# Eight more tokens gathered row by row, waits reordered, and half of a query projection made for both token groups at once

## The chip, the cores and the metric

One core of a Trainium2 chip runs the whole kernel. The time is device microseconds of one execution. All data are fp32; a matrix multiplication of 128x128 weights shows as two LDWEIGHTS and two MATMUL records in the trace.

## What is computed

One layer of a decoder for 320 tokens: 256 of a prompt and 64 of eight requests (eight each). Cut to what matters here:

```python
def one_block(xb):                                    # PEER: product-key experts
    q = (xb @ w_pq).reshape(TOKEN_BLOCK, PEER_HEADS, PEER_DKEY)     # 8 heads x 256
    s1 = jnp.einsum('thd,kd->thk', q[..., :half], sub_k1)
    s2 = jnp.einsum('thd,kd->thk', q[..., half:], sub_k2)
    v1, i1 = lax.top_k(s1, PEER_TOPK)
    v2, i2 = lax.top_k(s2, PEER_TOPK)
    ...
    eidx = jnp.take_along_axis(cidx, pos, axis=-1)     # 16 of 16384 experts a head
    gate = jax.nn.softmax(best.astype(jnp.float32), axis=-1)
    u = expert_u[eidx]
    act = jax.nn.gelu(jnp.einsum('td,thkd->thk', xb, u).astype(jnp.float32), approximate=False)
    vv = expert_v[eidx]
    return jnp.einsum('thk,thkd->td', (gate * act).astype(xb.dtype), vv)
```

Before it come two attention mixers with an output projection (`w_out`), and cross-attention of four heads to 256 memory tokens (`w_cq`, `w_co`), each behind an RMSNorm; a final RMSNorm follows.

## The kernel before

Tokens are columns, 16 blocks of 128 features (`KT`). Group 0 (`FIRST_TILE`) is the first 128 tokens, group 1 (`THE_REST`) the other 192. Weights stream in chunks of 1 MB (128 x 2048) through a ring `WR` of four slots, loaded by SP in the order of `STREAM`; SP loads a slot again when PE has used it (`s_used`).

The stages, in PE's order:

- Projections and prompt attention, then request attention, eight iterations `n` (keys and values of a request are loaded by POOL into single buffers). Among the parts of an iteration PE makes the output tiles, cross queries and cross outputs of group 0 (`out_tile`, `cq_tile`, `co_tile` with group 0), into banks 5 and 6 by turns. DVE adds each to the residual stream in `XT` (`add_to_stream`, L891), behind `softmax_s(n + 1)`. `turn_s(n)` is the transposition of an iteration.
- Group 1: 16 `out` tiles, 4 `cq`, a loop over cross-attention (`scores_c`, `turn_c`, `values_c`, ten steps), 16 `co`. The query tiles of the experts for group 0 (`pq_tile(0, f)`, 16 of 128 columns) are set among them; those of group 1 (`pq_tile(1, f)`, 192 columns) follow. So each chunk of `w_pq` is loaded twice. The memory keys `km` and values `vm` of the requests come in two halves of four requests.
- Experts. For group 0 (128 tokens) every chosen expert row is fetched by an indirect DMA: row n of the list holds one expert for each of 128 partitions, 1 MB. POOL issues them (L539 for `expert_u`, L545 for `expert_v`), three or four in flight; DVE makes a dot product from each `u` row (`u_dot`, L1240) and adds each `v` row with its weight (`v_row`, L1253). There are 128 such rows for group 0. 16 more (`FEW`) hold the first 16 tokens of group 1, as 16 tokens x 8 heads on the partitions, with `h_few` as their input.
- The other 176 tokens (`DENSE`) go through all experts: 128 chunks of `uT` (`dense_u`, into four banks, gelu by ScalarE), then 128 chunks of `expert_v` (`dense_v`), 16 multiplications of 176 columns each. The gates are applied by maps: for chunks 100 to 123 (`MAP_LO` to `MAP_HI`) DVE makes one-hots (`one_hots`), PE multiplies them (`gate_maps`), DVE and ScalarE apply them, four tokens to a group. The choices of those tokens are transposed on PE at chunk 92 (`TURN`, `s_turn`); DVE copies them (`turned`, `s_turnev`) when it has done 141 row dots (`ROWS_BEFORE`), and the first map waits for this.
- In the maps DVE does one row dot or row sum a chunk, two at each third.
- The sum of the 16 tokens' rows is put into PSUM by 16 small multiplications with `pick` at `expert_v` chunk 96 (`FEW_OUT`).

Choosing the experts is DVE's work, in parts (`choose_part`: sub-keys, sums, experts) for one or two heads, set by hand between row dots (`next_row`). POOL can't issue a row before the experts of its heads are chosen (`s_idx`), nor rows 128 on before the choices of the 16 tokens were spread by ScalarE's DMAs (`s_few`), behind chunk 80.

Of the kernel before, what the change touches and what calls it, by code (L numbers as in the profile page):

```python
# [26 lines left out]
P = 128  # L27
D = 2048
# [28 lines left out]
FEW = 16  # L57
REST = NT - P
DENSE = REST - FEW
# [6 lines left out]
ROWS = SLOTS + FEW  # L66
# [10 lines left out]
FEW_OUT = 96  # L77
# [7 lines left out]
def tiles_of(stage, g, lo, hi):  # L85
# [69 lines left out]
def build(nc, d):  # L155
    with ExitStack() as ctx:
# [11 lines left out]
        BIG = region("BIG", NCH * DENSE + (URING + 2) * D)  # L168
# [84 lines left out]
        vm = [BIG[:, at:at + 1024] for at in (4096, 13440, 22528, 23552)]  # L253
# [4 lines left out]
        h_few = BIG[:, NCH * DENSE:NCH * DENSE + D]  # L258
        u_ring = [BIG[:, NCH * DENSE + (1 + r) * D:NCH * DENSE + (2 + r) * D] for r in range(URING)]
        h_tok = BIG[:, NCH * DENSE + (URING + 1) * D:NCH * DENSE + (URING + 2) * D]  # L260
# [43 lines left out]
        def tile_out(stage, g, f):  # L304
            if g == FIRST_TILE:
                at = f % 2 if stage == "pq" else 5 + f % 2
            else:
                at = (2, 3, 7)[f % 3] if stage in ("out", "co") else 2 + f % 2
            return bank[at][:, 0:WIDTH[g]]
# [58 lines left out]
        s_dev = sem("dense_gelu")  # L368
        s_vlast = sem("v_finished")
# [47 lines left out]
        def _(sp):  # L417
# [44 lines left out]
            def mem_values(g):  # L462
                for n in range(4):
                    sp.dma_start(vm[n], d["vm"][4 * g + n]).then_inc(s_vm[g], 16)

            for chunk in STREAM:
                pos, (stage, g, f) = POS[chunk], chunk
                before = pos - WR_N
                if before == POS["out", 1, 15]:
                    sp.wait_ge(s_used, FREED["out", 1, 15])  # L470
                    mem_keys(0)
                    mem_values(0)
                if before == POS["pq", 0, 10]:
                    sp.wait_ge(s_cS, V_REQ[0] + 1)
                    mem_keys(1)
                if before == POS["pq", 0, 12]:
                    sp.wait_ge(s_cV, 1)
                    mem_values(1)
# [23 lines left out]
        def _(pool):  # L502
# [28 lines left out]
            for n in range(ROWS):  # L531
# [3 lines left out]
                else:  # L535
                    pool.wait_ge(s_few, 16 * PH)
# [11 lines left out]
        def _(act):  # L548
# [160 lines left out]
            def keep_query(g, f):  # L709
# [27 lines left out]
            for k in range(2, 9):  # L737
                square(THE_REST, CROSS, k)
            for f in range(4, 8):
                keep_query(FIRST_TILE, f)  # L740
            for k in range(9, KT):
                square(THE_REST, CROSS, k)
                if k == 9:
                    keep_scores(2)
            keep_query(FIRST_TILE, 8)
            root(THE_REST, CROSS)
            keep_query(FIRST_TILE, 9)
            for it in range(7):
# [8 lines left out]
                if it < 4:  # L757
                    keep_query(FIRST_TILE, 10 + it)
            keep_scores(3)
            for k in range(KT):  # L760
                square(THE_REST, FFN, k)
            keep_query(FIRST_TILE, 14)
            root(THE_REST, FFN)
            keep_query(FIRST_TILE, 15)
            keep_scores(4)
            for f in range(KT):
                keep_query(THE_REST, f)
                if f == 1:
                    keep_rows(3, h_few, big)
            for c in range(OF_FIRST, len(GROUPS)):  # L770
# [1318 lines left out]
```

## Time and profile before

| | |
|---|---|
| median of 3 runs | 2308.41 us (2307.99 to 2311.57) |
| profiled execution, its own time | 2311.11 us |
| its span | 2309.2 us |
| TensorE busy | 2207.9 us, 96% |
| VectorE busy | 1179.1 us, 51% |
| ScalarE busy, GpSimd busy | 301.2 us, 386.3 us |
| moved by DMA | 843.21 MB, mean 365 GB/s |
| mean granted TensorE clock | 0.984 |

Busy time of PE counts each matmul to its modelled end, so PE looks busy also where it goes on slowly. A stretch is read from its DMA share, the number of PE records in it and who waits for whom.

### The profile page before, as it was taken

Reading aid. Unit: us, or ns where it says so; the run is one execution under the profiler, and the core shown is the slowest. Engines: PE = TensorE matmul, PEld = TensorE weight load, DVE = VectorE, ACT = ScalarE, POOL = GpSimd, SP = SyncE. Lnnn points to the kernel's source line nnn. Section 1 sums busy time; section 2 is a strip of 40 time slices with the busy share of each in tenths; the row PEclk is TensorE's granted clock in tenths of the full one; section 3 lists DMA queues with packets and bytes.
Section 4 is the critical chain, followed back from the end, with each engine's and each line's share of the span. In section 5 each row is a group of like instructions: output and inputs, shape, how many; then the busy total and the mean of one; then the engine's idle time right before and its main releaser. Section 6 shows DMA issues by size and latency. Waiting matters only on the chain.

```text
span 2309.2 us, 35404 instructions
## 1 busy us (share of the span) xinstructions
PE 2207.9 (96%) x14282; PEld 2015.7 (87%) x14282; DVE 1179.1 (51%) x2095; ACT 301.2 (13%) x926; POOL 386.3 (17%) x414
## 2 busy tenths in 40 slices
PE   7999998789889879999999999999999999999998
PEld 5677776577589868999999999899999999999998
DVE  3200003833566647767777544599744444444422
ACT  2000001722221012011111110144200000000000
POOL 0100000022302011232212221133311111111100
PEclk9999999999999989999999999999999999999999
DMA  7999982289959898999999999999999999999974
GB/s 280 405 413 381 385 316 81 80 333 357 398 201 396 345 383 315 407 398 422 422 421 420 420 420 420 372 372 376 402 422 421 422 422 421 422 422 422 421 315 155
DMA packets 117787, 843.21 MB, mean 365 GB/s; under 512 B 14432, under 2 KB 16608, under 8 KB 30656
## 3 DMA queue, kind: packets, MB, share of 16 engines
q1 hardware_dynamic: 62752, 485.30, 52.4%
q0 software_dynamic: 54128, 354.58, 37.7%
q10 hardware_dynamic: 816, 2.11, 0.2%
q8 instruction: 58, 0.95, 0.2%
q14 instruction: 33, 0.27, 0.0%
HBM read 834.25 MB, written 74.78 MB: 394 GB/s over the span
## 4 chain that ended last, share of the span: by engine, by line
PE 64%; DMA 23%; DVE 8%; issue 2%; ACT 1%; POOL 1%; SPq 0%; DVEq 0%; POOLq 0%; ACTq 0%
PE low L1414 39%; PE big L1414 24%; DMA BIG<-expert_u,VB 20%; DVE BIG L1240 4%; DMA WR<-wall 1%; DMA BIG<-kaT 1%; ACT BIG L630 1%; DMA BIG<-expert_v,VB 1%; DMA BIG<-memT 0%; DMA BIG<-va 0%; DVE CST L968 0%; POOL BIG L525 0%; DVE BIG L846 0%; PE low L1538 0%; DVE HT L883 0%
## 5 line engine op out<-in xcount | busy, mean ns | idle before, releaser
L1414 PE MATMUL low<-HT,WR 128*128 128x176 f32 (+3 forms) x6336 | 1081.9, 333 | 8.4 <-DMA WR<-wall 7.0
L1414 PEld LDWEIGHTS low<-HT,WR 128*128 128x128 f32 x6336 | 984.2, 191 | 98.2 <-issue 9.7
L1414 PE MATMUL big<-BIG,WR 128*128 (+3 forms) x2888 | 450.7, 312 | 11.3 <-DVE XT L891 7.1
L1253 DVE SCALAR_TENSOR_TENSOR XT<-BIG,VB,XT 128x2048 f32<-128x2048 f32 x128 | 300.9, 2351 | 302.7 <-DMA BIG<-expert_v,VB 302.4
L1414 PE MATMUL low<-BIG,WR 128*128 (+3 forms) x2616 | 434.8, 321 | 12.6 <-DMA WR<-wall 10.3
L1414 PEld LDWEIGHTS big<-BIG,WR 128*128 128x128 f32 x2888 | 419.3, 193 | 30.1 <-issue 18.5
L1240 DVE SCALAR_TENSOR_TENSOR BIG<-BIG 128x2048 f32<-128x2048 f32 x144 | 329.5, 2291 | 210.8 <-DMA BIG<-expert_u,VB 209.7
L1414 PEld LDWEIGHTS low<-BIG,WR 128*128 128x128 f32 x2616 | 411.0, 192 | 17.8 <-issue 10.5
L539 POOL DMA_INDIRECT BIG<-expert_u,VB x144 | 161.5, 1122 | 683.8 <-DVE BIG L1240 609.5
L545 POOL DMA_INDIRECT BIG<-expert_v,VB x144 | 161.5, 1122 | 558.2 <-DVE XT L1253 477.3
L914 DVE TENSOR_SCALAR BIG<-low 128x320 f32 x32 | 15.7, 492 | 264.0 <-PE low L1414 264.0
L1414 PE MATMUL big<-BIG 128*32 128x256 f32 (+4 forms) x868 | 80.5, 376 | 16.1 <-issue 8.9
L1414 PEld LDWEIGHTS big<-BIG 128*32 128x32 f32 (+2 forms) x868 | 52.7, 141 | 36.5 <-issue 14.6
L777 ACT ACTIVATE BIG<-low 128x176 f32 x100 | 31.8, 318 | 334.3 <-PE low L1414 324.2
L819 ACT ACTIVATE HT<-XT 128x2048 f32<-128x2048 f32 x1 | 1.9, 1910 | 557.1 <-DVE XT L1253 557.1
L793 ACT ACTIVATE HT<-HT,VB 128x128 f32<-128x128 f32 x176 | 56.2, 390 | 89.9 <-DVE HT L1354 89.9
L1354 DVE TENSOR_TENSOR HT<-CST,VB 128x512 f32<-128x512 f32 x88 | 56.6, 684 | 7.7 <-PE big L1414 7.7
L1414 PE MATMUL big<-HT 128*128 128x128 f32 x352 | 47.9, 280 | 5.0 <-ACT HT L793 5.0
L1414 PEld LDWEIGHTS big<-HT 128*128 128x128 f32 x352 | 45.5, 194 | 5.6 <-issue 5.5
L511 POOL DMA_DIRECT2D HT<-kbT x1 | 0.5, 536 | 266.8 <-PE low L1414 266.8
L525 POOL DMA_DIRECT2D BIG<-kaT x56 | 29.8, 539 | 81.2 <-PE low L1414 81.2
L622 ACT ACTIVATE BIG<-low 128x512 f32<-128x512 f32 (+3 forms) x5 | 2.3, 466 | 293.3 <-PE low L1500 293.3
(230 smaller groups left out, 1124.0 us busy)
## 6 DMA issues: line engine op xcount, KB each, us to landing
WR<-uT SPq DMA_DIRECT2D x128, 1024.0 KB
WR<-expert_v SPq DMA_DIRECT2D x128, 1024.0 KB
WR<-wall SPq DMA_DIRECT2D x122, 1024.0 KB
BIG<-va POOLq DMA_DIRECT2D x48, 512.0 KB, 11.0
BIG<-kaT POOLq DMA_DIRECT2D x64, 384.0 KB, 11.0
BIG<-kmT SPq DMA_DIRECT2D x2, 2048.0 KB, 12.9
BIG<-vm SPq DMA_DIRECT2D x8, 512.0 KB, 13.4
XT<-xT SPq DMA_DIRECT2D x1, 2560.0 KB, 21.9
```

What stands on the lines that cost most here:

```text
L525: pool.dma_start(kr[j][:, NEWK:SW], d["kaT"][n, j, :, FIRST:PAST]).then_inc(s_kr[j], 16)
L539: nc.gpsimd.indirect_dma_start(u_ring[n % URING], None, d["expert_u"], bass.IndirectOffsetOnAxis(eidx[:, n:n + 1], 0)).then_inc(s_ug[n % U ...
L545: nc.gpsimd.indirect_dma_start(v_ring[n % VRING], None, d["expert_v"], bass.IndirectOffsetOnAxis(eidx[:, v_slot(n):v_slot(n) + 1], 0)).the ...
L622: nc.scalar.activation(VT[0:m, t, q * 512:q * 512 + w], bank[3 + n % 2][0:m, 0:w], ACT.Copy).then_inc(s_vtev, 1)
L630: ins = nc.scalar.activation(pb[:, s, lo:hi], pb[:, s, lo:hi], ACT.Exp, bias=stat[:, c:c + 1], scale=1.0, accum_out=stat[:, c + 4:c + 5])
L777: nc.scalar.activation(C[:, bass.ds(i * (UB * DENSE) + r * DENSE, DENSE)], u_out[r], ACT.Gelu).then_inc(s_dev, 1)
L793: nc.scalar.activation(x, x, ACT.Copy, scale=turned[2][:, 4 * g + j:4 * g + j + 1]).then_inc(s_weighed, 1)
L914: nc.vector.tensor_scalar(QK[:, bass.ds(i * (4 * NT) + r * NT, NT)], bank[r % 2][:, 0:NT], 1.0, None, ALU.mult).then_inc(s_ev, 1)
L1240: nc.vector.scalar_tensor_tensor(out=u, in0=u, scalar=1.0, in1=h_tok if n < SLOTS else h_few, op0=ALU.mult, op1=ALU.mult, accum_out=dots[: ...
L1253: nc.vector.scalar_tensor_tensor(out=x_tok, in0=rows_of(row), scalar=weight, in1=x_tok, op0=ALU.mult, op1=ALU.add).then_inc(s_vsum, 1)
L1354: ins = nc.vector.tensor_tensor(hot[z][g % 2], iota.unsqueeze(1).broadcast_to([P, 4, NKEY]), turned[z][:, 4 * g:4 * g + 4].unsqueeze(2).br ...
L1414: return nc.tensor.matmul(out, lhsT, rhs, start=start, stop=stop, skip_group_check=True)
```

## The change

Four things.

1. `FEWER = 8` more tokens of group 1 are gathered. They are laid 8 tokens x 16 (eight heads, two halves of the 16 choices) on the partitions, so that 8 more `u` rows and 8 more `v` rows hold them: `ROWS` is 152. The dense part has 168 columns. Their input is made in `h_tok` once the 128 first dots are done, and transposed by PE at chunk 92 behind `s_turnev`; ScalarE issues 16 more small DMAs for their choices. Their sum takes a second pick. The first pick moves from `expert_v` chunk 96 to 32, the second is at 96.
2. `pq_tile(0, 8..15)` is dropped; `pq_tile(1, f)` for f from 8 is made with all 320 columns, first of the sixteen. Choosing and scoring of heads 2 to 7 moves back.
3. In the request attention DVE adds the tiles before `softmax_s(n + 1)`; the cross output of group 0 has a third bank from f = 6.
4. `vm` of the second half has places of its own; two of its loads are issued with the first half.

```diff
-DENSE = REST - FEW
+ALONE = FEW + FEWER
+DENSE = REST - ALONE
-ROWS = SLOTS + FEW
+ROWS = SLOTS + FEW + FEWER
+V_FEW = (*range(SLOTS, SLOTS + FEW), *range(40), *range(SLOTS + FEW, ROWS), *range(40, SLOTS))
-FEW_OUT = 96
+FEW_OUT, FEWER_OUT = 32, 96
...
-         + tiles_of("out", 1, 0, 9) + tiles_of("pq", 0, 4, 8) + tiles_of("out", 1, 9, 16) + tiles_of("pq", 0, 8, 10)
-         + tiles_of("cq", 1, 0, 4) + tiles_of("pq", 0, 10, 14) + tiles_of("co", 1, 0, 16) + tiles_of("pq", 0, 14, 16)
-         + tiles_of("pq", 1, 0, 16))
+         + tiles_of("out", 1, 0, 16) + tiles_of("pq", 0, 4, 6) + tiles_of("cq", 1, 0, 4) + tiles_of("pq", 0, 6, 8)
+         + tiles_of("co", 1, 0, 16) + tiles_of("pq", 1, 8, 16) + tiles_of("pq", 1, 0, 8))
...
-                at = f % 2 if stage == "pq" else 5 + f % 2
+                at = f % 2 if stage == "pq" else (5, 6, 0)[(f - 6) % 3] if stage == "co" and f >= 6 else 5 + f % 2
...
-                if before == POS["out", 1, 15]:
+                if before == POS["cq", 1, 0]:
                     sp.wait_ge(s_used, FREED["out", 1, 15])
                     mem_keys(0)
-                    mem_values(0)
+                    mem_values(0, 0, 4)
+                    mem_values(1, 0, 2)
-                if before == POS["pq", 0, 10]:
+                if before == POS["pq", 0, 6]:
                     sp.wait_ge(s_cS, V_REQ[0] + 1)
                     mem_keys(1)
-                if before == POS["pq", 0, 12]:
+                if before == POS["pq", 0, 7]:
                     sp.wait_ge(s_cV, 1)
-                    mem_values(1)
+                    mem_values(1, 2, 4)
...
-                act.dma_start(chosen[FEW * h:FEW * (h + 1), :, SLOTS:ROWS], few_src[:, :, h * PK:(h + 1) * PK]).then_inc(s_few, 16)
-            dense_gelu(TAIL, MAP_LO)
+                act.dma_start(chosen[FEW * h:FEW * (h + 1), :, SLOTS:SLOTS + FEW], few_src[:, :, h * PK:(h + 1) * PK]).then_inc(s_few, 16)
+                for half in range(2):
+                    to, k = half * 64 + h * FEWER, h * PK + half * FEWER
+                    act.dma_start(chosen[to:to + FEWER, :, SLOTS + FEW:ROWS], fewer_src[:, :, k:k + FEWER]).then_inc(s_few, 16)
+            dense_gelu(TAIL, TURN)
+            keep_rows(4, h_tok, big)
+            dense_gelu(TURN, MAP_LO)
...
-                if n + 1 < REQ:
-                    softmax_s(n + 1)
-                for f in (*with_scores, *with_turn):
+                for f in with_scores:
                     add_to_stream(FIRST_TILE, CROSS, f)
...
+                if n + 1 < REQ:
+                    softmax_s(n + 1)
+                for f in with_turn:
+                    add_to_stream(FIRST_TILE, CROSS, f)
...
-                if 10 <= k <= 12:
-                    choose_part(2, k - 10)
-                if k < 9 or k in (13, 14):
+                if k < 15:
                     next_row()
...
-                if k in (3, 6, 9, 12):
+                if k == 8:
                     next_row()
...
+            for part in range(3):
+                choose_part(2, part)
+                next_row()
             while row[0] < ROWS_AHEAD:
...
+                if n == SLOTS - 1:
+                    dve.wait_ge(s_udot, SLOTS)
+                    nc.vector.tensor_copy(h_tok.rearrange("p (k h t) -> p k h t", k=KT, h=P // FEWER), HT_by[:, :, P + FEW:P + ALONE].unsqueeze(2).broadcast_to([P, KT, P // FEWER, FEWER])).then_inc(s_rep, 1)
...
+                cols = slice(0, NT) if stage == "pq" and g == THE_REST and f >= 8 else COLS[g]
...
             ins.then_inc(s_turn, 1)
+            pe.wait_ge(s_turnev, 1)
+            pe.wait_ge(s_rep, 2)
+            turn_rows(h_tok, P)
             u_chunks(TURN, MAP_LO)
...
-                    pe.wait_ge(s_turnev, 1)
+                    pe.wait_ge(s_ht, 4)
...
+            v_chunks(FEW_OUT, FEWER_OUT)
+            pe.wait_ge(s_vsum, FEWER_AT + FEWER)
+            for k in range(KT):
+                mm(v_all[k][:, FEW:ALONE], h_few[:, k * P:(k + 1) * P], pick_fewer, start=False, stop=True)
+            v_chunks(FEWER_OUT, MAP_LO)
```

## Rows read from the trace of the kernel before

**Rows 1.** The page's part 2, 40 slices of 57.7 us.

```profile
PEclk9999999999999989999999999999999999999999
DMA  7999982289959898999999999999999999999974
```

**Rows 2.** Stretches: length, busy time (records) of each engine, clock, DMA share, GB/s.

```profile
462.00:520.00 58.00, 51.66 (x487) 42.34 (x487) 23.48 (x83) 11.76 (x34) 15.90 (x30) 1.00 0.85 333
520.00:577.00 57.00, 52.31 (x502) 43.67 (x506) 18.04 (x66) 11.55 (x33) 15.13 (x29) 0.91 0.91 357
577.00:635.00 58.00, 49.24 (x483) 33.13 (x479) 30.91 (x113) 14.07 (x47) 17.98 (x35) 1.00 1.00 398
...
789.00:828.00 39.00, 31.20 (x194) 30.64 (x193) 15.87 (x35) 2.62 (x5) 3.74 (x4) 0.87 0.94 371
828.00:874.00 46.00, 32.59 (x284) 24.75 (x284) 27.78 (x58) 8.05 (x25) 9.46 (x8) 0.89 1.00 407
997.00:1398.00 401.00, 401.00 (x2689) 400.80 (x2688) 267.77 (x533) 54.58 (x108) 90.20 (x78) 1.00 1.01 418
1398.00:1480.00 82.00, 81.93 (x544) 79.72 (x544) 37.37 (x33) 5.40 (x17) 15.95 (x17) 1.00 1.01 421
1510.00:1645.00 135.00, 134.92 (x976) 134.63 (x976) 130.37 (x160) 55.75 (x223) 48.99 (x29) 1.00 0.98 389
1645.00:2135.00 490.00, 489.73 (x3165) 471.78 (x3164) 232.12 (x104) 2.76 (x6) 97.22 (x100) 1.00 1.01 422
```

**Rows 3.** Timeline of POOL and DVE in 1719 to 1726: start, us, what.

```profile
1720.06 0.94 POOL L545 DMA_INDIRECT BIG<-expert_v,VB  x1 [4.04 <-DVE XT L1253]
1722.41 2.35 DVE L1253 SCALAR_TENSOR_TENSOR XT<-BIG,VB,XT 128x2048 f32<-128x2048 f32 x1 [2.62 <-DMA BIG<-expert_v,VB]
1725.04 0.94 POOL L545 DMA_INDIRECT BIG<-expert_v,VB  x1 [4.04 <-DVE XT L1253]
```

**Rows 4.** DVE from 1659 on: its group of row sums, then two timeline rows.

```profile
L1253 DVE SCALAR_TENSOR_TENSOR XT<-BIG,VB,XT 128x2048 f32<-128x2048 f32 x113 | 265.7, 2351 | 298.0 <-DMA BIG<-expert_v,VB 298.0
...
2219.47 2.35 DVE L1253 SCALAR_TENSOR_TENSOR XT<-BIG,VB,XT 128x2048 f32<-128x2048 f32 x1 [2.63 <-DMA BIG<-expert_v,VB]
2289.20 2.41 DVE L1397 TENSOR_TENSOR XT<-XT,big 128x192 f32<-128x192 f32 x8 [67.38 <-PE big L1414]
```

**Rows 5.** Timeline of DVE and PE around the first gate map.

```profile
1479.44 2.29 DVE L1240 SCALAR_TENSOR_TENSOR BIG<-BIG 128x2048 f32<-128x2048 f32 x1 [2.67 <-DMA BIG<-expert_u,VB]
1485.50 1.83 PE L1414 MATMUL big<-HT 128*128 128x128 f32 x7 [4.95 <-ACT HT L793]
```

**Rows 6.** Groups of POOL in 0 to 997: its row fetches.

```profile
L539 POOL DMA_INDIRECT BIG<-expert_u,VB x49 | 54.4, 1111 | 303.4 <-DVE BIG L1240 242.8 <-DVE VB L1227 54.1 <-issue 6.5
```

**Rows 7.** Timeline of PE in the request attention, the tiles behind a stop.

```profile
520.69 8.99 PE L1414 MATMUL big<-BIG,WR 128*128 128x128 f32 x64 [3.53 <-DVE XT L891]
...
552.39 10.15 PE L1414 MATMUL big<-BIG,WR 128*128 128x128 f32 x64 [3.53 <-DVE XT L891]
...
600.78 3.84 PE L1414 MATMUL big<-BIG,WR 128*128 128x128 f32 x32 [3.54 <-DVE HT L1073]
```

**Rows 8.** The chain in time; then timelines of PE, DVE, POOL in 692 to 906.

```profile
75.96 292.87 PE low L1414 x1088
...
715.22 5.20 PE big L1414 x32
...
840.79 3.57 PE low L1414 x32
...
808.65 18.55 PE L1414 MATMUL low<-HT,WR 128*128 128x192 f32 x96 [6.99 <-DMA WR<-wall]
...
865.12 3.64 PE L1414 MATMUL big<-BIG 128*32 128x512 f32 x16 [8.89 <-issue]
...
902.65 1.35 DVE L875 RECIPROCAL BIG<-BIG 128x192 f32<-128x192 f32 x1 [4.39 <-ACT BIG L597]
...
786.42 0.94 POOL L539 DMA_INDIRECT BIG<-expert_u,VB  x1 [31.74 <-DVE BIG L1240]
```

More of the change, by code:

```diff
@@ L257, in build @@
         C_by = C.rearrange("p (c t) -> p c t", t=DENSE)
-        h_few = BIG[:, NCH * DENSE:NCH * DENSE + D]
-        u_ring = [BIG[:, NCH * DENSE + (1 + r) * D:NCH * DENSE + (2 + r) * D] for r in range(URING)]
-        h_tok = BIG[:, NCH * DENSE + (URING + 1) * D:NCH * DENSE + (URING + 2) * D]
+        h_few = BIG[:, ROOM:ROOM + D]
+        u_ring = [BIG[:, ROOM + (1 + r) * D:ROOM + (2 + r) * D] for r in range(URING)]
+        h_tok = BIG[:, ROOM + (URING + 1) * D:ROOM + (URING + 2) * D]
         v_ring = u_ring + [h_tok]
@@ L368, in build @@
         s_dev = sem("dense_gelu")
+        s_fewout = sem("few_added")
         s_vlast = sem("v_finished")
@@ L736, in _ @@
             keep_scores(1)
-            for k in range(2, 9):
+            for k in range(2, KT):
                 square(THE_REST, CROSS, k)
[L739 to L745, printed above, removed]
+            keep_query(FIRST_TILE, 4)
             root(THE_REST, CROSS)
-            keep_query(FIRST_TILE, 9)
+            keep_query(FIRST_TILE, 5)
             for it in range(7):
@@ L1238, in u_dot @@
                 dve.wait_ge(s_ug[n % URING], 16 * (n // URING + 1))
+                if n == SLOTS + FEW:
+                    dve.wait_ge(s_ht, 4)
                 u = u_ring[n % URING]
-                nc.vector.scalar_tensor_tensor(out=u, in0=u, scalar=1.0, in1=h_tok if n < SLOTS else h_few, op0=ALU.mult, op1=ALU.mult, accum_out=dots[:, n:n + 1]).then_inc(s_udot, 1)
+                nc.vector.scalar_tensor_tensor(out=u, in0=u, scalar=1.0, in1=h_few if SLOTS <= n < SLOTS + FEW else h_tok, op0=ALU.mult, op1=ALU.mult, accum_out=dots[:, n:n + 1]).then_inc(s_udot, 1)
             def v_row(n):
@@ L1329, in _ @@
                     if not later:
-                        first = slice(0, FEW)
+                        first = slice(0, ALONE)
                         link(nc.vector.scalar_tensor_tensor(out=eidx_f[first], in0=exp_f[1][0][first], scalar=float(NKEY), in1=exp_f[1][1][first], op0=ALU.mult, op1=ALU.add))
@@ L1695, in values_c @@
                         for n in range(4):
-                            ins = mm(bank[5][32 * n:32 * n + 32, :], pT[:, b * P + 32 * n:b * P + 32 * n + 32], vm[n][:, b * 512:(b + 1) * 512], start=(b == 0), stop=(b == 1))
+                            ins = mm(bank[5][32 * n:32 * n + 32, :], pT[:, b * P + 32 * n:b * P + 32 * n + 32], vm[r][n][:, b * 512:(b + 1) * 512], start=(b == 0), stop=(b == 1))
                     ins.then_inc(s_cV, 1)
@@ L1906, in dense_v @@
                         pe.wait_ge(s_dev, NCH - UB + k // 2 + 1)
-                    ins = mm(v_all[k][:, FEW:REST], WR[:, slot_of(r) * D + k * P:slot_of(r) * D + (k + 1) * P], coefs, start=(first and k % 2 == 0), stop=last)
+                    ins = mm(v_all[k][:, ALONE:REST], WR[:, slot_of(r) * D + k * P:slot_of(r) * D + (k + 1) * P], coefs, start=(first and k % 2 == 0), stop=last)
                     if last:
```

127 lines of the change are left out of this document (70 added, 57 removed).

## The prediction

> **What bounds the kernel now.** I read the page's slices first: TensorE's clock is full almost everywhere and so is the DMA, from the fifteenth slice to the last but two [rows 1]. So the question of every stretch is which of the two is late, and the table of stretches answers it [rows 2]. I call L the expert dots (997 to 1659 us, matrix chunks of `uT`, 128 of them, 32 matmul records each) and M the expert sums (1659 to 2294, chunks of `expert_v`). In 997 to 1398 PE issues one record each 149.1 ns (401 us, x2689), so a chunk takes 4.77 us, with no idle. In 1645 to 2135 the DMA moves 422 GB/s, which is its level everywhere it is full, and a chunk takes 4.97 us: the row gathers are issued by POOL once in 4.98 us and DVE, which needs 2.35 us for a row, waits 2.6 us for the next one each time [rows 3]. One chunk and one row are 1 MB each, so a load costs 4.975/2 = 2.49 us whoever asks for it. M is thus bound by DMA until its last row at 2221.8 [rows 4], and by PE after it; L is bound by PE until about 1398 and then by DMA: 1398 to 1480 moves 421 GB/s and its share is 1.01. PE idles 5 us just before 1485.5, when it starts on the gate maps, and the last row dot before it (the 141st) ended at 1481.7 [rows 5]. In the maps, 1510 to 1645, DVE is busy 130.4 of 135 us [rows 2], so it sets that pace together with PE.
>
> The check that I use below: from 997 to 1481.7 the DMA loads 100 chunks (104 less the 4 that lay in the ring) and 96 rows (49 were issued by 997, of which some 47 had landed [rows 6]; 143 by the end). 196 loads x 2.49 = 488 us, against 484.7 measured. So counting loads tells when a row is done in L.
>
> **The change, part by part.** Base: the profiled execution, span 2309.2, its own time 2311.1; the median of the runs, 2308.4, is 0.8 under the span.
>
> *Attention (462 to 692).* With two banks, the second output tile behind `turn_s(n)` waits until DVE has added the tile two before it, and DVE does that behind `softmax_s(n+1)`, 3.4 us long. The rows show it: PE stops at 517 and 549 and restarts at 520.7 and 552.4 for DVE L891, and at 600.8 for L1073, 3.53 us each; the two tiles behind the stop took 8.99 and 10.15 us [rows 7] where 64 such records at full clock take 7.1 (3.57 us for 32 [rows 8]). I put the surplus to half clock (1.2 of 2.4 GHz). The new order adds those tiles first: it gives back 3.5+1.6, 3.5+2.8 and 3.5 = 15 us, plus 1 to 2 from the third bank of the cross output (DVE's squares of tiles 0 to 8 stay on that path, so no more). What could take it back is DMA: share 0.85, 0.91, 1.00 in 462 to 635 [rows 2], idle capacity 9+5 = 14 us up to 577 and none after; the key and value loads of requests 5 to 7 are issued only when their buffers come free. Bounds 8 and 17; I take 13 gained.
>
> *Query projection and cross-attention (692 to 997).* Removed from PE: eight 128-wide tiles (3.57 us each [rows 8]), 28.6 us; the eight tiles that replace them are 320 wide, at 269.2 ns a record (292.87 us for 1088 [rows 8]) 8.62 us each instead of 5.20 (192 wide, 32 records, 162.5 ns [rows 8]), +27.4 us. PE's work falls by 1.2 us. Eight chunk loads fall away, 20 us of DMA, in a stretch that PE waits for DMA: 7.0 us before 808.65 and 8.9 us before 865.12, the second logged as issue; I read it as the second memory-value load, two of whose four parts now come early [rows 8]. With the half clock (0.87 and 0.89 in 789 to 874 [rows 2]) the two cost some 20 us. But the 128-wide tiles also filled waits, and these open:
> the first eleven output tiles have eleven row dots beside them, then four to six more follow where before DVE chose experts in the time of the moved tiles. At one row per 4.97 us the 17th dot ends some 5 us before the old end of the stretch (789), not 14 before it: 6 to 7 us of cover lost. Five mem loads now stand ahead of the chunk of query tile 6, which makes it 3 to 4 us late, and the second key load stands behind four chunks, 3 us late. In the cross loop two fewer fillers leave a DVE chain of at least one row (2.3 us) an iteration: 46 us becomes about 42. Behind the cross output nothing covers the FFN norm (DVE idled 4.39 us before its inverse at 902.65, itself 1.35 us [rows 8]), so 4 to 5 us idle for PE, and 2 us of half clock. Summed from 692 to the projection: some 184 us of PE work at full clock before, 28.6 gone, and now some 35 of idle and half clock in place of 30: the projection starts near 882 instead of 906, and L starts 27.4 + 3.8 (two key scores moved in, half clock, norm waits) after that: 1001 instead of 997. So +4; bounds: -12 if the idle found now vanishes and only half of the new kind comes, +10 if the tile-6 chunk and the keys are both a full pair of loads (5 us each) late. Work on choosing for heads 2 and 3 moves behind the FFN norm (row 32 can't be fetched before it, as POOL waits for its index; the like kept DVE from its dots and POOL idle for 31.74 us at row 14, tiles among it [rows 8], and I estimate 19 for DVE's work alone), but rows run at DVE's pace, 4.2 us, under the wide tiles, since these need a chunk only each 8.6 us. I get 52 rows landed at L's start instead of 47.
>
> *L: narrower chunks, and a wait moved forward.* 168 columns: 149.1 less half of (162.5 - 149.1) = 142.4 ns, 4.56 us a chunk, 0.21 less. On 128 chunks that is 27 us if PE sets the pace. But rows and chunks share the DMA: at 4.975 us a pair, PE can't go below 4.95 for long (in 997 to 1398 it used 84 chunks and spent a lead of three: 401/81), only until its ring of four is spent. So PE reaches chunk 92 at about (92-3) x 4.95 = 441 us after L's start, hardly earlier than before. There the change puts `wait s_turnev` in front of `turn_rows(h_tok)`, and DVE raises it only behind its 141st dot. Before, that wait stood behind chunk 100. By the count of loads the 141st dot now comes after 92 chunks (96 less 4) and 91 rows, 183 x 2.49 = 456 us, plus some 4 us as row 128 can't be fetched until ACT has issued 24 small DMAs instead of 8 behind chunk 80: 460. PE stands still 15 to 20 us; the ring fills meanwhile. Then two copies, the transposes (16 records of 111.6 ns, 1.8 us at full clock, twice that at half), some 3 us of half clock, and eight chunks at 4.56: the maps start at 507, where before they started at 1485.5 - 997 = 488.5. Behind the moved wait stand those eight chunks, which used to hide it: +18. It takes 2 us off that the short half clock of before at the maps is gone. The maps have 42 groups for 44: by PE alone 24 x 0.21 + 2 x 8 x 0.112 = 6.8 us less; but DVE is full there, and only the two groups' share of it goes, so I take 3.3, half. Sum of L: +12.7. Bounds: with 47 rows landed at the start instead of 52, +12 more; with 58, 15 less, but no better than -3, which is the stretch with the stop fully gone.
>
> **A rule of the Trainium skill.** M's rows show one chunk and one row per 4.97 us, that is, equal halves [rows 3]. The Trainium skill, "DMA: Bandwidth & Descriptors", section "Queues, rings and completion order", says that each DMA engine serves the queues with work in turn, a packet each. The trace agrees in M, where both queues always hold work; in L to 1398 chunks got more than half (4.77 us each), as only three rows are in flight there. By the rule alone PE would gain nothing from narrow chunks in L and M; by PE's rate alone 54 us in both.
>
> *M and the end.* Eight more rows there, and eight fewer of its rows run in the maps, since the eight more dots use DVE's places: 129 rows are left at M's start for 113 [rows 4]. At 4.975 each the last would end at 562.8 + 79.6 = 642 us after M's start; the chunk loads end near 617 (124 x 4.975, four lie in the ring), and the last rows then come at DVE's 2.35, so about 634. Narrow chunks buy nothing before that (DMA-bound), and PE ends with them: floor 128 x 4.56 + two picks of 5 (32 records at 111.6 ns and some half clock, an estimate) = 594, by DMA 627. Before, DVE's closing adds began at 2289.2, 630.2 after M's start [rows 4]. So +4, and 2 more because ScalarE's square of the first tile (2 us by estimate, a pass like DVE's 2.35), long done before, now stands on the closing chain. The extra picks hide in the DMA-bound stretch; if that cover is gone they cost 5. I take +5; bounds -8 (rows end first, PE's end at 622) and +12 (no speed-up at the end).
>
> Sum: -13 + 4 + 12.7 + 5 = +8.7, span 2318, less 0.8: 2317; I put it at **2316**.
>
> **Rivals.**
> 1. *The stop in L is longer.* Fewer rows have landed by L's start than I say (POOL held at row 32 for the 19 us of choosing), 47 as before: 12 us more, 2328; with M at its bound 2334. For it: rows stood still for 31.74 us at row 14 for the like choosing [rows 8]. Against it: the light DMA under the wide tiles.
> 2. *The other side: DMA relief in 692 to 997 wins.* If eight fewer loads let rows and chunks come without waits there, the stretch gives 12 instead of costing 4, L starts 985 rather than 1001 (attention apart), and the sum is 2300; with attention at its bound of 17, 2296. It decides if the projection tiles start by 872. For it: 20 us of loads are gone from a stretch that is at share 0.94 to 1.00 [rows 2]. Against: row dots and the DVE chain bound the out tiles and the cross loop at once behind it.
> 3. *No change that can be told:* the attention's gain and L's stop cancel, as they do if L costs 6 rather than 12.7 and M nothing: 2304 to 2313. The 5 rows of lead decide.
> 4. *The narrowing counts in full* (chunks are served first): 54 less the stop, near 2275. M's locked pace speaks against it.
>
> **How the numbers follow.** Forecast 2310 to 2322: 0.32; rival 1: 0.22; rival 3: 0.21; rival 2: 0.20; rival 4: 0.05. A change under 0.2% (4.6 us) is about what this measurement can't tell from none. Over 2313: 0.32 of which nine tenths, and rival 1, 0.50; within, 0.23; under 2303.8, 0.27. The range leaves out rival 4 and the worst of 1: 2294 to 2333; the likeliest case alone is 2310 to 2322.
>
> **What would show it.** Right: no stop of PE for L891 behind `turn_s`, L's start within 10 us of 988 (attention's gain taken off); a PE gap of 10 to 25 us at chunk 92 ending with DVE's copies of `turned`, and none at chunk 100; M at 4.97 us a chunk almost to its end, last row within 10 us of PE's end. Wrong: chunks in M under 4.9 us while rows flow; no gap at chunk 92; the cross loop under 35 us.

## The result, and the profile after

The changed kernel took 2341.35 us, median of 4 runs (2338.50 to 2347.68), against 2308.2 of the kernel before (4 runs, 2305.15 to 2311.57): ratio 1.0139, 95% interval 1.0122 to 1.0156. It is 33 us slower. I had forecast 2316 in 2294 to 2333: the sign was right, the size a quarter of what came, and the time lies outside the range.

The profiled execution of the changed kernel has a span of 2337.4 us, 28.2 over the one of before. Its slices, to be read beside [rows 1]:

```profile
PEclk9999999999999889999999997899999999999999
DMA  7999962299869974999999999689999999999997
```

Before, no slice behind the fifteenth had a low clock. Here two have, the 25th and 26th (1403 to 1519 us), and the DMA is low in the 26th and 27th: for a while neither of the two is fully used. The stretches, as in [rows 2] (length, busy time and records of PE, PE's loads, DVE, ACT, POOL, then clock, DMA share, GB/s):

```profile
462.00:577.00 115.00, 109.12 (x1050) 87.08 (x1054) 50.80 (x181) 23.53 (x68) 33.90 (x64) 0.99 0.94 371
...
799.00:873.00 74.00, 51.56 (x356) 42.85 (x355) 42.31 (x99) 15.01 (x41) 8.52 (x10) 0.88 0.85 338
...
996.00:1398.00 402.00, 396.65 (x2723) 388.15 (x2722) 267.91 (x532) 54.09 (x110) 90.00 (x77) 1.00 1.01 420
1398.00:1431.00 33.00, 32.69 (x234) 32.01 (x233) 13.68 (x13) 2.18 (x7) 4.70 (x5) 1.00 0.93 379
1431.00:1469.00 38.00, 0.29 (x8) 0.15 (x3) 24.75 (x29) 0.00 (x0) 14.62 (x11) 0.53 0.86 330
1469.00:1510.00 41.00, 40.93 (x274) 40.93 (x275) 2.51 (x5) 4.06 (x8) 0.24 (x1) 0.94 0.65 232
1510.00:1665.00 155.00, 152.57 (x1137) 151.90 (x1136) 142.78 (x188) 65.13 (x259) 44.98 (x31) 1.00 0.93 366
1679.00:2150.00 471.00, 458.23 (x3062) 439.40 (x3061) 220.45 (x96) 1.80 (x3) 89.03 (x95) 0.99 1.01 422
```

Three things stand in it. In 996 to 1398 PE fits 2723 records into 402 us, against 2689 in 401 before: narrower chunks, and little faster: 4.72 us a chunk (402 us over 2723/32) where PE alone would need 4.56, with the DMA at 1.01. In 1431 to 1469 PE does nothing. In 1679 to 2150 it is 422 GB/s again, and PE is idle 13 us. The timeline names the stop (start, us, what; in brackets the idle time before it and who ended it), PE first, then DVE:

```profile
1430.56 0.73 PE L1438 MATMUL big<-CST,HT 64*64 64x64 f32 x12
1469.07 3.67 PE L1794 MATMUL big<-CST,BIG 128*128 128x128 f32 x16 [37.78 <-DVE VB L1369]
1472.54 2.71 PE L1438 MATMUL low<-HT,WR 128*128 128x168 f32 x12
...
1512.70 1.05 PE L1438 MATMUL big<-HT 128*128 128x128 f32 x8
```

```profile
1464.88 2.29 DVE L1256 SCALAR_TENSOR_TENSOR BIG<-BIG 128x2048 f32<-128x2048 f32 x1 [0.17 <-DMA BIG<-expert_u,VB]
...
1468.79 0.23 DVE L1369 COPY VB<-big 64x64 f32<-64x64 f32 x1
```

L1369 is the last copy of `turned`, which DVE makes behind its 141st dot (1464.88 to 1467.10), and L1794 is `turn_rows(h_tok)`, now ahead of chunk 92. So the stop is the one forecast, in its place and with its releaser, but 38 us long where I had 15 to 20. The first gate map starts at 1512.7; before it started at 1485.5 [rows 5].

Where the 28.2 us come from, stretch by stretch of the two traces:

```
stretch                                forecast   measured
up to the first row fetch (attention)   -13        -9.9    (692.3 -> 682.4)
from there to the expert dots (L)        +4        +8.5    (L starts 997.0 -> 995.6)
L                                       +12.7     +21.4    (662.0 -> 683.4)
M and the end                            +5        +8.2    (650.2 -> 658.4)
sum                                      +8.7     +28.2
```

### The profile page after: what moved, and what is told of

The parts are those of the page before. It is cut to its first block, busy times and chain, and to the rows that moved or that the text cites. A ratio compares the mean times of both kernels' runs of the same rounds, so it can differ in the third digit from the quotient of the medians.

```text
span 2337.4 us, 35000 instructions
## 1 busy us (share of the span) xinstructions
PE 2178.8 (93%) x14058; PEld 1948.2 (83%) x14058; DVE 1214.1 (52%) x2115; ACT 297.1 (13%) x917; POOL 401.2 (17%) x430
## 4 chain that ended last, share of the span: by engine, by line
PE 42%; DMA 40%; DVE 11%; issue 4%; ACT 2%; POOL 1%; SPq 0%; DVEq 0%; POOLq 0%; ACTq 0%
PE low L1438 34%; DMA BIG<-expert_v,VB 25%; PE big L1438 7%; DMA BIG<-expert_u,VB 7%; DMA WR<-uT 4%; DVE XT L1272 3%; DVE BIG L1256 2%; DMA BIG<-kaT 2%; DMA WR<-wall 1%; DVE HT L1378 1%; DMA BIG<-va 1%; ACT BIG L637 1%; DVE BIG L1270 1%; DMA BIG<-memT 0%; DVE BIG L1388 0%
## 5 line engine op out<-in xcount | busy, mean ns | idle before, releaser
L1438 PE MATMUL low<-HT,WR 128*128 128x168 f32 (+3 forms) x6104 | 1065.6, 336 | 14.4 <-DMA WR<-wall 5.4
L1438 PEld LDWEIGHTS low<-HT,WR 128*128 128x128 f32 x6104 | 941.3, 192 | 131.5 <-issue 21.2
L1256 DVE SCALAR_TENSOR_TENSOR BIG<-BIG 128x2048 f32<-128x2048 f32 x152 | 347.5, 2291 | 198.6 <-DMA BIG<-expert_u,VB 197.3
L1438 PE MATMUL big<-BIG,WR 128*128 (+3 forms) x2888 | 436.0, 306 | 15.3 <-DMA WR<-expert_v 7.7
L1438 PEld LDWEIGHTS big<-BIG,WR 128*128 128x128 f32 x2888 | 404.9, 192 | 39.7 <-issue 38.2
L1438 PE MATMUL low<-BIG,WR 128*128 (+3 forms) x2616 | 420.6, 316 | 14.2 <-DMA WR<-wall 9.3
L1438 PEld LDWEIGHTS low<-BIG,WR 128*128 128x128 f32 x2616 | 398.3, 192 | 19.3 <-issue 9.3
L546 POOL DMA_INDIRECT BIG<-expert_u,VB x152 | 179.7, 1182 | 744.6 <-DVE BIG L1256 596.8
L552 POOL DMA_INDIRECT BIG<-expert_v,VB x152 | 158.2, 1041 | 592.0 <-DVE XT L1272 488.8
L782 ACT ACTIVATE BIG<-low 128x168 f32 x100 | 30.9, 311 | 325.6 <-PE low L1438 299.9
L1270 DVE SCALAR_TENSOR_TENSOR BIG<-BIG,VB 128x2048 f32<-128x2048 f32 x22 | 51.7, 2349 | 20.5 <-DMA BIG<-expert_v,VB 20.1
```

The lines of the kernel that those rows point to most:

```text
L546: nc.gpsimd.indirect_dma_start(u_ring[n % URING], None, d["expert_u"], bass.IndirectOffsetOnAxis(eidx[:, n:n + 1], 0)).then_inc(s_ug[n % U ...
L552: nc.gpsimd.indirect_dma_start(v_ring[n % VRING], None, d["expert_v"], bass.IndirectOffsetOnAxis(eidx[:, v_slot(n):v_slot(n) + 1], 0)).the ...
L782: nc.scalar.activation(C[:, bass.ds(i * (UB * DENSE) + r * DENSE, DENSE)], u_out[r], ACT.Gelu).then_inc(s_dev, 1)
L1256: nc.vector.scalar_tensor_tensor(out=u, in0=u, scalar=1.0, in1=h_few if SLOTS <= n < SLOTS + FEW else h_tok, op0=ALU.mult, op1=ALU.mult, a ...
L1270: nc.vector.scalar_tensor_tensor(out=h_few, in0=row, scalar=weight, in1=h_few, op0=ALU.mult, op1=ALU.add).then_inc(s_vsum, 1)
L1438: return nc.tensor.matmul(out, lhsT, rhs, start=start, stop=stop, skip_group_check=True)
```

## The experiments

All ratios are against the kernel before, run on the same chip. The table gives what each trace shows: the start of L, how long after it POOL fetches row 143 (it may when the 141st dot is done, and does so some 1 us behind it; the column "dot 141"), PE's stop before `turn_rows` or the first map, the length of L, and the length from M's start to the end of the span. Each row is one trace: e5 and e6 have the same instructions up to L, and their L starts differ by 5.5 us, so a difference of that size between two traces tells little by itself.

```
kernel                      median  ratio [95%]             L at   dot 141  stop   L      M+end
before                      2308.2  1                        997.0  485.4    5.3   662.0  650.2
changed                     2341.4  1.0139 [1.0122,1.0156]   995.6  472.7   38.0   683.4  658.4
e1 wait back                2317.3  1.0034 [1.0021,1.0047]   994.9  488.8   17.8   663.0  658.4
e2 choices at 72            2335.6  1.0118 [1.0093,1.0142]   995.1  471.5   34.2   680.3  659.5
e3 both                     2311.1  1.0017 [1.0003,1.0030]   992.2  478.9    4.0   652.1  656.3
e4 attention only           2301.2  0.9964 [0.9946,0.9982]   988.1  485.9    3.6   661.9  652.0
e5 + projection             2301.4  0.9961 [0.9945,0.9977]   995.2  480.6    2.2   655.0  649.8
e6 + narrow, no rows        2295.8  0.9940 [0.9923,0.9956]  1000.7  479.9    2.6   650.8  645.5
e7 attention, choices 72    2301.4  0.9964 [0.9955,0.9974]   989.7  483.6    3.6   658.0  651.9
e8 attention + tokens       2306.9  0.9990 [0.9976,1.0003]   986.0  485.0    6.5   657.1  660.9
e9 attention, pick at 32    2298.6  0.9948 [0.9928,0.9968]   990.0  482.8    3.0   658.9  649.2
e10 projection, pick at 32  2302.7  0.9966 [0.9952,0.9980]   997.3  480.4    1.7   654.8  649.3
e11 e3 once more            2305.9  one run                  995.4  479.3    3.4   649.9  658.8
```

**e1: the wait put back.**

```diff
-            pe.wait_ge(s_turnev, 1)
-            pe.wait_ge(s_rep, 2)
-            turn_rows(h_tok, P)
             u_chunks(TURN, MAP_LO)
+            pe.wait_ge(s_turnev, 1)
+            pe.wait_ge(s_rep, 2)
+            turn_rows(h_tok, P)
```

ScalarE's `keep_rows(4, h_tok, big)` moves behind `dense_gelu(TAIL, MAP_LO)` in the same way.

> The changed kernel with the wait for DVE's copies of the turned choices, and the eight-token transposes behind it, put back behind chunk 99 (ScalarE's copy of them too). Theory: the stop of 38 us that PE had at chunk 92 is waiting for the 141st row dot, and eight chunks of 4.6 to 5.0 us can run in that time. The dot itself then comes later than now (471 us after L's start), as the chunks take loads again: 92 rows and 96 chunk loads at 2.49 us are 468, and some 12 for the hold at row 128 make 480. PE stops 5 to 12 us at chunk 100, the maps start 14 to 26 us earlier, the kernel takes 2316 to 2327 us, and M stays at 4.97 us a chunk. Rival: the loads alone set when the dots end, so that the eight chunks only move the stop; then the time stays at 2337 to 2342.

Measured 2317.31, 24 us under the changed kernel, and L is 20.4 us shorter: the theory's direction and size. The dot came later than the 480 expected (487.9, row 143 fetched at 488.8), so a stop of 17.8 us is left where 5 to 12 were expected, now at chunk 100:

```profile
1459.71 7.57 PE L1437 MATMUL low<-HT,WR 128*128 128x168 f32 x52
1484.74 3.68 PE L1793 MATMUL big<-CST,BIG 128*128 128x128 f32 x16 [17.45 <-DVE VB L1368]
```

**e2: the choices spread earlier.** One number, with which POOL isn't held at row 128:

```diff
-EXPS, TAIL = 64, 80
+EXPS, TAIL = 64, 72
```

> The changed kernel with one number different: ScalarE spreads the few tokens' choices behind chunk 72 instead of behind chunk 80, so that POOL doesn't stand at row 128 (16.8 us in the changed kernel). Theory: the hold made the 141st dot 9 to 12 us later than the count of loads says, so PE's stop at chunk 92 falls from 38 to 26 to 29 us, and the time by 8 to 12 us, to 2329 to 2333. Rival: chunk loads used the DMA in the hold, and the rows only changed places with them; then the stop shrinks by under 4 us and the time stays within 4 of 2341.

Measured 2335.58. The theory fell. POOL's gap at row 128 went from 17.7 to 5.0 us, and it fetched row 143 only 1.2 us earlier (472.7 to 471.5 after L's start); the 141st dot itself ended 0.8 us earlier. The stop shrank by 3.8 us, as the rival has it, mostly because PE reached it 2.9 us later; the time fell by 6 us, a little more than the rival allows. In the changed kernel, POOL's fetches around the hold and the stop are:

```profile
1394.59 0.94 POOL L546 DMA_INDIRECT BIG<-expert_u,VB  x1 [4.05 <-DVE BIG L1256]
1412.31 0.94 POOL L546 DMA_INDIRECT BIG<-expert_u,VB  x1 [16.78 <-DMA VB<-HT]
...
1441.62 0.94 POOL L546 DMA_INDIRECT BIG<-expert_u,VB  x1 [4.02 <-DVE BIG L1256]
1445.36 2.51 POOL L546 DMA_INDIRECT BIG<-expert_u,VB  x1 [2.80 <-DVE BIG L1256]
...
1462.86 2.67 POOL L546 DMA_INDIRECT BIG<-expert_u,VB  x1 [3.13 <-DVE BIG L1256]
...
1468.30 0.94 POOL L546 DMA_INDIRECT BIG<-expert_u,VB  x1 [0.30 <-issue]
```

During the hold the chunk loads use the DMA (378 GB/s in 1394 to 1412), so what is lost is small, and the rows catch up later, in PE's stop. From 1441.6 on the ring of chunks is full and only rows are loaded: eight in 26.7 us, 3.34 each, faster than the 4.97 of a shared DMA but slower than the 2.49 per load of my count. The windows of that time, the changed kernel's first, then that of e2:

```profile
1441.00:1468.00 27.00, 0.00 (x0) 0.00 (x0) 19.19 (x21) 0.00 (x0) 12.04 (x8) 0.50 0.80 293
1394.00:1412.00 18.00, 17.46 (x119) 16.70 (x118) 8.13 (x7) 0.93 (x3) 0.94 (x1) 1.00 0.94 378
```

```profile
1394.00:1412.00 18.00, 17.65 (x121) 16.89 (x120) 8.92 (x9) 0.93 (x3) 4.11 (x4) 1.00 1.01 421
1440.00:1467.00 27.00, 0.00 (x0) 0.00 (x0) 17.16 (x20) 0.00 (x0) 11.60 (x8) 0.50 0.76 288
```

Rows alone move 288 to 293 GB/s in the mean, not 422. The mean has two parts, as smaller windows of the changed kernel show:

```profile
1450.00:1460.00 10.00, 0.00 (x0) 0.00 (x0) 5.94 (x7) 0.00 (x0) 2.81 (x3) 0.50 0.95 354
1446.20:1449.00 2.80, 0.00 (x0) 0.00 (x0) 1.05 (x3) 0.00 (x0) 2.50 (x2) 0.50 0.28 85
1464.20:1466.20 2.00, 0.00 (x0) 0.00 (x0) 1.83 (x3) 0.00 (x0) 1.70 (x2) 0.50 0.00 0
```

With three rows in flight they move 354 GB/s, and in two gaps next to nothing; both gaps lie where a fetch took POOL 2.5 us or more (1445.36, 1462.86) and not 0.94. At 422 GB/s the 27 us lost 8.3 us of loads, some 4.2 of them in the gaps. Whether it is POOL's slow fetches or the few rows in flight that keep this queue from filling the DMA was not tested; POOL's times are rough, too.

**e3: both.**

> Both edits together: the wait back behind chunk 99, and the choices spread behind chunk 72. Theory: the two costs of L add up nearly, since one is PE waiting and the other DMA standing idle: 92 rows and 96 chunk loads at 2.49 us put the 141st dot at 468 to 474 us after L's start, when PE is at the end of chunk 98 or 99, so that PE's stop at chunk 100 is under 6 us; the time is 2310 to 2317, that is 24 to 31 under the changed kernel. Rival: they are one cost seen twice, and the two together give no more than the better of them alone.

Measured 2311.05, 30 under the changed kernel, and the stop is down to 4.0 us, both as the theory has it, though the dot came at 478.0 and not by 474. With the wait at chunk 100 the hold at row 128 costs 9.9 us of dot time (488.8 against 478.9), with the wait at chunk 92 it cost 1.2. In the first case chunk loads take their half to the end (in e1 the last eight rows are fetched 4.97 us apart), so that a row that is late stays late; in the second PE's stop gives the rows the DMA, at 3.34 us a row, and they catch up. In e3 the DMA is full up to the stop, and the stop is short:

```profile
1398.00:1468.00 70.00, 68.56 (x469) 65.43 (x468) 33.47 (x30) 4.36 (x14) 13.49 (x14) 1.00 1.01 422
1468.00:1472.00 4.00, 0.44 (x4) 0.19 (x2) 3.93 (x11) 0.31 (x1) 0.94 (x1) 0.86 1.02 424
```

**e4: the attention's part alone.** The core of its diff, in DVE's loop over the requests:

```diff
-                if n + 1 < REQ:
-                    softmax_s(n + 1)
-                for f in (*with_scores, *with_turn):
+                for f in with_scores:
                     add_to_stream(FIRST_TILE, CROSS, f)
...
+                if n + 1 < REQ:
+                    softmax_s(n + 1)
+                for f in with_turn:
+                    add_to_stream(FIRST_TILE, CROSS, f)
```

> The kernel before with the attention's part of the change alone: DVE adds the output tiles behind the turned outputs before the next request's softmax, and the last ten of the first tile's cross-output tiles use three banks. Theory: it gives the 9.9 us that the changed kernel gains by the first tile of the second group, and nothing behind takes it back, since everything behind starts that much earlier: 2297 to 2300 us. Rival: from 692 us on the DMA is at share 0.94 to 1.00 and sets the time whenever PE comes, so that an earlier start is waited away and the time stays within 4 us of 2308.

Measured 2301.19, ratio 0.9964: 8 us faster, nearly as expected (2297 to 2300), and the rival fell. L starts at 988.1 and is as long as before (661.9). The stops behind `turn_s` that [rows 7] show are gone but for one. PE's waits in 462 to 692 of this kernel:

```profile
PE low L1418 <- DMA BIG<-kaT: 5.9, 11, 1.8
PE big L1418 <- DMA BIG<-va: 3.9, 6, 1.1
PE big L1418 <- DVE XT L891: 2.6, 1, 2.6
```

It now waits 9.8 us in all for the loads of keys and values of the requests, where it waited 3.8 before; so some of what the new order gives is waited away there.

**e5: and the query projection's part, without the eight tokens.** In the edit of the tiles below, 176 columns and 144 rows are kept, and the choices and the first map's wait are as before:

```diff
-         + tiles_of("out", 1, 0, 9) + tiles_of("pq", 0, 4, 8) + tiles_of("out", 1, 9, 16) + tiles_of("pq", 0, 8, 10)
-         + tiles_of("cq", 1, 0, 4) + tiles_of("pq", 0, 10, 14) + tiles_of("co", 1, 0, 16) + tiles_of("pq", 0, 14, 16)
-         + tiles_of("pq", 1, 0, 16))
+         + tiles_of("out", 1, 0, 16) + tiles_of("pq", 0, 4, 6) + tiles_of("cq", 1, 0, 4) + tiles_of("pq", 0, 6, 8)
+         + tiles_of("co", 1, 0, 16) + tiles_of("pq", 1, 8, 16) + tiles_of("pq", 1, 0, 8))
```

> The kernel before with the attention's part and the query projection's part of the change, without the eight more tokens (176 dense columns, 144 rows, the first map's wait behind chunk 99 as before). Theory: the projection's part makes the expert dots start 5 to 6 us later than with the attention's part alone (994 against 988), and gives back 1 to 4 of it, since one or two more rows have landed by then and PE's stop of 3.6 us at chunk 100 goes: 2302 to 2308 us, against 2301 for the attention alone. Rival (the relief of 20 us of chunk loads): the dots start at 985 or earlier and the time is under 2298.

Measured 2301.44, just under what was expected: no difference from the attention alone. L starts 7.1 us later (995.2), and L is 6.9 us shorter, so that it ends at 1650 us in both. The rows are not ahead for it: by 995.2 us POOL had fetched 51 of them in e4 as well as in e5 (49 by e4's own start of L), and the 141st dot ended at 1473.2 in e4, at 1474.9 in e5. PE makes up its later start in L, where the loads set the pace: of L's records it had issued 3232 by 1473 us in e4 and 3214 in e5, 18 apart, where 7.1 us at its own pace are 48. The eight chunk loads saved buy no time that these traces show.

**e6: narrower chunks without their price.** e5 with `FEW, FEWER = 16, 8` in the dense widths only; the eight tokens get no rows and no expert output.

> As the projection's kernel, but the matrix chunks take 168 columns for 176 (42 map groups for 44), and the eight tokens left out of them get no expert output at all: no rows are gathered, dotted or summed for them. This is the narrowing without its price. Theory: rows and chunks share the DMA, so that a chunk goes on taking 4.97 us wherever rows flow; only the maps (3 us) and the last chunks of the sums, behind the last row (some 15 x 0.21 = 3 us), get faster: 4 to 9 us less than the projection's kernel. Rival (narrowing counts in full): 256 x 0.21 us and the maps, 50 to 55 us less.

Measured 2295.84, 5.6 us under e5, as the theory has it; the rival is out by 45. (The intervals of the two ratios overlap a little, so 5.6 is rough.) The same 408 us of the sums, in e5 and then in e6:

```profile
1712.00:2120.00 408.00, 407.84 (x2627) 391.50 (x2627) 192.84 (x82) 0.00 (x0) 75.87 (x81) 1.00 1.01 422
```

```profile
1712.00:2120.00 408.00, 395.83 (x2629) 375.31 (x2628) 193.21 (x83) 0.00 (x0) 76.80 (x82) 1.00 1.01 422
```

As many records, the same 422 GB/s, and PE idle 12 us for 0: here its gain is all waited away.

**e7 and e8.** e7 is e4 with `TAIL = 72`; e8 is e3 without the projection's part.

> The kernel with the attention's part alone, and ScalarE's spreading of the few tokens' choices moved from behind chunk 80 to behind chunk 72. Theory: with eight small transfers and not 24, POOL wasn't held at row 128 (5.0 us between the rows there, as everywhere), so that nothing is gained: within 3 us of the attention alone, 2298 to 2304. Rival: a hold too short to see costs the 3.6 us for which PE waits at chunk 100, and the time is under 2298.

Measured 2301.36, as the attention alone: no hold, nothing to gain.

> The kernel before with the attention's part and the eight more tokens, in the better of the forms tried so far (wait behind chunk 99, choices behind chunk 72), and the query projection left as before. Theory: the projection's part costs 5 to 6 us up to the expert dots and gives little back, so that this is 2 to 6 us under the kernel with all parts in that form (2311): 2305 to 2309, still above the attention alone (2301), since eight more rows cost 40 us of DMA in the sums and the narrower chunks give back only what stands behind the last row. Rival: the eight chunk loads saved are what lets the rows keep up, and without them PE's stop grows: 2314 or more.

Measured 2306.93, inside the expected span. By the ratios it is 6 us under e3 (0.9990 for 1.0017) and 6 over e4 and e7 (0.9964). So with the eight tokens the projection's part costs some 6 us, where e5 against e4 has nothing; the sums of the stretches don't show it (e8's span is 2304.0 us, e3's 2300.6, e11's 2304.1), so this belongs to what stays open under e11. PE's stop grew from 4.0 to 6.5 us, a trace of the rival, but L starts 6 us earlier.

**e9 and e10: the transposes of the gathered sums behind chunk 32**, one number (`FEW_OUT = 96` to `32`) in e4 and in e5.

> The kernel with the attention's part alone, and one number of before changed: the transposes that add the 16 gathered tokens' sums run behind chunk 32 of the expert sums, not behind chunk 96 (the rows they wait for are done by chunk 16). Theory: behind chunk 96 nothing hides them, since PE runs at its own 4.77 us a chunk from there to the end, and they cost 5.2 us and some half clock; behind chunk 32 the DMA is what PE waits for, and the chunk loads run on in their time. What stays is that chunks 96 to 108 then go at 4.97 again, 2 to 3 us. So 2 to 5 us less than the attention alone: 2296 to 2299. Rival: the chunk loads can't run ahead in their time, as rows take the DMA, and the 5 us are lost there as well: within 1.5 us of 2301.

> The same move of the transposes to chunk 32 in the kernel with the attention's and the projection's part. Theory: as there, 2 to 5 us less than without it: 2296 to 2300. Rival: no gain, 2300 to 2303.

PE at the transposes, in e4 and then in e9:

```profile
2126.32 1.85 PE L1418 MATMUL low<-VB,BIG 128*128 128x16 f32 x16
2128.02 2.30 PE L1418 MATMUL big<-VB,BIG 128*128 128x16 f32 x16
2130.16 5.04 PE L1418 MATMUL big<-BIG,WR 128*128 128x176 f32 x16
2134.99 3.18 PE L1418 MATMUL low<-BIG,WR 128*128 128x176 f32 x16
```

```profile
1806.99 1.85 PE L1418 MATMUL low<-VB,BIG 128*128 128x16 f32 x16
1808.69 1.94 PE L1418 MATMUL big<-VB,BIG 128*128 128x16 f32 x16
1810.48 4.31 PE L1418 MATMUL big<-BIG,WR 128*128 x16
```

The transposes and the slow records behind them take as long behind chunk 32 as behind chunk 96. But in 1815 to 2125 us, behind them, e9's PE issues 2029 records where e4's issues 1996 at the same 422 GB/s: it makes up a chunk. e9's M is 2.8 us shorter than e4's, e10's only 0.5 shorter than e5's; the medians moved by -2.6 and +1.2, the ratios by -0.0016 and +0.0005, with overlapping intervals. e10 is also 4 us over e9 (0.9966 for 0.9948), again with overlapping intervals: its L starts 7.3 us later and is only 4.1 us shorter. Whether the move gains anything isn't settled. e9 is the fastest complete kernel here, 0.9948 of before and 0.9812 of the changed one (0.9948/1.0139).

**e11: e3 once more.**

> The kernel with all parts, the wait behind chunk 99 and the choices behind chunk 72, once more: its profiled execution took 2302.4 us and was the fastest of ten, whose median is 2311. If the missing 8 us are an ordinary scatter of the whole, this execution's parts differ from the first one's a little everywhere; if they have a place, one of the three stretches (up to the expert dots, dots, sums) is 5 to 10 us longer and the others are within 2.

2305.89 us. L starts 3.2 us later than in e3's first trace, L is 2.2 shorter, M 2.5 longer: an ordinary scatter. That doesn't explain why e3's ten runs have a median of 2311, when its two traces and e5's say that it should be within some 4 us of e5's 2301. None of e3's longer executions was traced; this stays open.

## Why the prediction was wrong, point by point

**Right:** what bounds each stretch, and where the change would bite. M's chunks stayed at 4.97 us while rows flowed, 129 rows were left at M's start as counted, L was bound by loads, the stop came at chunk 92, ended with DVE's copies, and there was none at chunk 100. e6 shows the narrowing by itself to be worth 5.6 us of the 54 of PE's work. The moved wait was named as the largest single loss.

**Wrong:** all four sizes, and all on one side, 19.5 us of span together. (The other 6 between 2316 and 2341 are that the median of the changed kernel's runs is 4.0 us over its profiled span, where I had taken 0.8 under it, and a rounding.)

*L, 8.7 of them; this is the step that failed.* "183 x 2.49 = 456 us, plus some 4 us": the dot ended at 471.5 us after L's start, not at 460, and the first map started at 517, not at 507. Two things account for the dot. POOL had fetched 51 rows by L's start, of which some 49 had landed, not 52: three loads, 7.5 us (rival 1's mechanism, at half its size). And a load costs 2.49 us only where both queues hold work. In the stop eight rows took 3.34 us each, 6.8 us more than counted. 456 + 7.5 + 6.8 = 470; the hold at row 128, for which I had 4, was worth 1 (e2). That this comes so near to 471.5 is partly luck: the same count was 3 us over for the kernel before, and 5 over for e3 (100 chunks and 94 rows, 483 for 478). The stop itself began 5 us earlier than I had it (435.7 for 441); without the hold, in e2, it began at 438.6. With 2 us for DVE's copies it was 38 us and not 15 to 20. My price for the moved wait, 18 us, was near the truth all the same: e1 gives 20.4 us in L and 24 in the medians. Behind the stop, PE's clock was at its lower level for 41 us, from 1433 to 1474, so only the transposes and the next few records paid for it, the 1.8 us for them becoming 3.67.

*The projection, 4.5.* The projection tiles started where I said (883.4 for 882, attention's gain taken off); from there to L it took 122.1 us, not 119, and the "+4" was 8.5. e5 against e4 has it at +7.1. That is inside my bounds. And 3 us of the miss are a slip in adding: the projection tiles at 882, the 91 us from there to L before, 27.4 and 3.8 make 1004, not the 1001 that I wrote; the terms themselves say 122.2 us, which is what the trace has. What I didn't see is that a later start of L is made up in L while the loads pace it (e5 against e4); in the changed kernel PE stood in its stop either way.

*Attention, 3.1.* Forecast -13, measured -9.9, in e4 -8.9. (The surpluses of 1.6 and 2.8 us in the forecast are taken from 7.4 us for a pair of tiles; from the 7.1 written beside them they would be half a us more.) What takes the rest is mostly what I had named, the DMA. PE waits in the changed kernel:

```profile
PE low L1438 <- DMA BIG<-kaT: 5.4, 9, 1.8
PE big L1438 <- DMA BIG<-va: 2.9, 5, 0.6
PE big L1438 <- DVE XT L901: 2.6, 1, 2.6
```

8.3 us for keys and values, for 3.8 before, at DMA share 0.94 in 462 to 577, and a cross-output tile that waits once.

*M, 3.2.* I had DVE's closing adds 634 us after M's start; they began at 638.1 (2317.09 less 1679.0). I had the chunk loads end at 617 and the last rows come quickly behind them. But in 2304 to 2308, 629 us after M's start, the chunks' queue still moved half of the packets (119 of 233). So rows and chunks end together, and only the last three rows come in one piece, hard before the adds:

```profile
2305.22 2.35 DVE L1272 SCALAR_TENSOR_TENSOR XT<-BIG,VB,XT 128x2048 f32<-128x2048 f32 x1 [2.62 <-DMA BIG<-expert_v,VB]
2309.88 7.29 DVE L1272 SCALAR_TENSOR_TENSOR XT<-BIG,VB,XT 128x2048 f32<-128x2048 f32 x3 [2.31 <-DMA BIG<-expert_v,VB]
2317.09 2.20 DVE L1421 TENSOR_TENSOR XT<-XT,big 128x192 f32<-128x192 f32 x8
```

The adds wait for DVE's own rows now, and no longer for PE as they did before [rows 4]. The 2 us that I gave to ScalarE's square were 0.3: from the adds to the end it takes 20.3 us, before 20.0.

None of the rivals reaches the measured time: the first, which has the right side and part of the cause, gives 2334 with M at its bound. The sum of my own worst bounds does (-8, +10, +24.7 and +12 make +38.7, 2347): the range of 2333 took it for granted that not all would go wrong together.

So the change in order: the attention's part gains 8 us (e4); the projection's part nothing (e5) or costs some 4 to 6 (e10 against e9, e3 against e8); the eight tokens cost 16 us net (e5 to e1: 8.0 in L and 8.6 in M by the traces, 15.9 by the medians), their rows 22 of loss and the narrowing 6 of gain (e6); the wait moved forward costs 24 more. The 16 hold the hold at row 128: with the choices spread at chunk 72 the tokens cost 10 (e5 to e3; 13 by the ratios) or 6 us (e7 to e8).

The rule of equal turns that the Trainium skill states ("DMA: Bandwidth & Descriptors", "Queues, rings and completion order") held where both queues always had work (4.97 us a row beside a chunk in M, in L from 1360 on, and even in e1's stop while the ring refilled).

## What to carry to other kernels

Where two streams share a full DMA, count loads, not engine time: making one engine's share cheaper moved 5.6 us of 54. But check the count where one stream stops, since the other may not be able to use the whole DMA. A wait that is moved ahead of a block of work costs the block, unless what it waits for was done by then; so ask when the awaited event happens (here the dot ended 36 us after PE got there) before looking at what the wait makes possible. And a range has to be held against the sum of the terms' bounds: here four errors, none out of its own bounds and all on one side, made 19.5 us, and a slip in adding was one of them.

## What the runs showed of the hardware

Row fetches alone, three in flight, moved 288 to 293 GB/s at DMA share 0.76 to 0.80 (354 at 0.95 between POOL's slow fetches), against 422 at 1.01 when chunk loads of another queue ran beside them (the changed kernel, e2). The same late transfer cost 1.2 us where the other queue paused afterwards and 9.9 us where it didn't (changed against e2, e1 against e3). In the changed kernel PE's granted clock fell to 1.2 GHz 2.0 us after PE had stopped, and was back at 2.4 GHz 5.1 us after work began again, 41.0 us at the lower level around a stop of 38.0; the stop of 17.8 us in e1 had 20.5 us at that level, the one of 4.0 us in e3 had 6.8, and the one of 3.6 us in e4 had 3.4, while around the equally long one in e7 the clock stayed at 2.4 GHz.
